# ScalarE scales the recurrence's keys as it evicts the projections, and two more tensors go through DRAM

## What is computed

```python
r, k, v = einsum(x_rkv, w_rkv)
w = -softplus(-(w0 + tanh(mix(3) @ w1) @ w2)) - 0.5
a = sigmoid(a0 + (mix(4) @ a1) @ a2)
g = sigmoid(mix(5) @ g1) @ g2
kk = heads(k * k_k)
kk = kk * rsqrt(max(sum(kk * kk), 1e-24))
k = k * (1.0 + (a - 1.0) * k_a)
y = _wkv7_scan(heads(r), exp(-exp(w)), heads(k), heads(v), kk, heads(a))
```

## Time and profile before

| what | us |
|---|---|
| median of the three runs | 2966.8 |
| lowest and highest run | 2958.1, 2972.0 |
| span of the profiled execution | 2962.6 |
| of it the projections of layer 1 | about 370 |
| of it the recurrence, from the first load to the last z | about 501 |
| busy: TensorE, VectorE, Pool, ScalarE | 2651.2, 1679.0, 1251.1, 931.4 |

### The profile page before, as it was taken

One profiled execution on the slowest core, in us unless ns is written; L12 is line 12 of the kernel. 1 busy time (PEld: TensorE's weight loads), 2 busy tenths in 40 slices (PEclk: granted clock), 3 DMA queues, 4 the chain that ended last, 5 costly groups with the idle time before them and its releaser, 6 DMA issues. The chain is left out here.

```text
span 2962.6 us, 48409 instructions
## 1 busy us (share of the span) xinstructions
PE 2651.2 (89%) x20064; PEld 2172.5 (73%) x20064; DVE 1679.0 (57%) x2078; ACT 931.4 (31%) x1551; POOL 1251.1 (42%) x630
## 2 busy tenths in 40 slices
PE   1887888999999999989989488888799999999999
PEld 1565667788887788767778377777687888788887
DVE  6745455655554633467963689998435443433434
ACT  2434433321224222154544233333234222222221
POOL 2532234444445444344433334444355444444443
PEclk9989999999999999999999799999899999999999
DMA  6421224354533222256566444433232233223333
GB/s 244 159 82 37 93 79 156 128 178 157 184 128 100 86 93 99 81 147 167 146 171 157 107 96 98 98 90 82 87 123 91 86 107 93 92 93 100 99 96 124
DMA packets 299001, 343.32 MB, mean 116 GB/s; under 512 B 214560, under 2 KB 214688, under 8 KB 298784
## 3 DMA queue, kind: packets, MB, share of 16 engines
q1 hardware_dynamic: 298784, 340.23, 38.1%
HBM read 298.29 MB, written 40.89 MB: 114 GB/s over the span
## 5 line engine op out<-in xcount | busy, mean ns | idle before, releaser
L709 POOL TENSOR_TENSOR wl<-w,wh 128x1024 fp32r<-128x1024 f32 x367 | 906.3, 2475 | 1274.8 <-ACT wh L750 1274.6
L180 PE MATMUL ps<-hi,wh 128*128 128x512 f32 x2208 | 883.6, 400 | 22.3 <-ACT qk_raw L787 10.4
L182 PE MATMUL ps<-hi,wl 128*128 128x512 f32 x2208 | 868.7, 393 | 0.0
L181 PE MATMUL ps<-lo,wh 128*128 128x512 f32 x2208 | 868.5, 393 | 0.0
L750 ACT ACTIVATE wh<-w 128x1024 fp32r<-128x1024 f32 x367 | 387.0, 1056 | 703.9 <-DMA w<-in_ffn_w_in 528.0
L1021 DVE SCALAR_TENSOR_TENSOR xt<-ps,mod,xt 128x512 f32<-128x512 f32 x384 | 286.6, 750 | 411.0 <-PE ps L182 404.5
L180 PEld LDWEIGHTS ps<-hi,wh 128*128 128x128 f32 x2208 | 420.3, 190 | 125.2 <-issue 33.8
L181 PEld LDWEIGHTS ps<-lo,wh 128*128 128x128 f32 x2208 | 421.0, 191 | 90.3 <-issue 3.7
L182 PEld LDWEIGHTS ps<-hi,wl 128*128 128x128 f32 x2208 | 419.6, 190 | 89.9
L1026 DVE TENSOR_TENSOR act<-ps,silu 128x512 f32<-128x512 f32 x88 | 60.9, 692 | 461.3 <-PE ps L182 461.3
L180 PE MATMUL ps<-act_hi,wh 128*128 128x512 f32 x704 | 282.4, 401 | 18.5 <-DVE act_lo L1030 10.0
(11 more groups left out here) (221 smaller groups left out, 3319.6 us busy)
## 6 DMA issues: line engine op xcount, KB each, us to landing
w<-in_ffn_w_in SPq DMA_DIRECT2D x176, 512.0 KB, 3.6
piece<-in_ada_w SPq DMA_DIRECT2D x96, 512.0 KB, 5.1
w<-in_ffn_w_out SPq DMA_DIRECT2D x88, 512.0 KB, 3.6
w<-in_w_rkv SPq DMA_DIRECT2D x48, 512.0 KB, 3.9
scratch<-silu SPq DMA_DIRECT2D x48, 256.0 KB, 3.0
scratch<-act SPq DMA_DIRECT2D x48, 256.0 KB, 3.1
w<-in_wqk SPq DMA_DIRECT2D x20, 512.0 KB, 5.4
xt<-in_xT SPq DMA_DIRECT2D x4, 2048.0 KB, 10.3
```

The source lines that it names most:

```text
L180: pe.matmul(out, w_hi(k), x_hi(k), start=first and k == 0, stop=False)
L181: pe.matmul(out, w_hi(k), x_lo(k), start=False, stop=False)
L182: ins = pe.matmul(out, w_lo(k), x_hi(k), start=False, stop=last and k == kc - 1)
L709: pool.tensor_tensor(wl[n % NW][:, :, :], wr[n % NW][:, :, :], wh[n % NW][:, :, :].bitcast(F32), ALU.subtract).then_inc(*wlo.up)
```

## The change

The products of the recurrence's keys with vectors move to the eviction of the projections.

In the projections: a k tile is evicted twice by ScalarE, once multiplied by `k_k` into the buffer `sq` and once plain; SyncE writes both, the first to `scratch` part 6. An a tile (`lora2`, `n % 3 == 1`) is evicted through the sigmoid, then, after a wait for that result, ScalarE makes (a * k_a - k_a) in a second buffer `a_gain`, and SyncE writes both, the second to `scratch` part 7. The two `a_gain` buffers are `total[0]` and a new tile. Buffers are free again when all writes from them have landed (`kept_before` counts them). VectorE makes -k_a once at the start.

In the recurrence: `begin` is gone from VectorE and `keys` from Pool. SyncE loads kk ready made right behind r, and `a_gain` into k2 right behind v. VectorE makes k2 = (a_gain + 1) * k in one instruction, `keys(x)`, right behind `bounded(x)`. `squares`, `decayed` and `bonus_terms` wait for both loads of the r semaphore, and `by_token(x, 0)`, `bonus_value` and `keys` for both of the v semaphore.

```diff
@@ projections: SyncE
 sp.dma_start(scratch_of(n % 3, n // 3, j), sg[i % 2]...).then_inc(*kept[i % 2].up)
+if n % 3 == 1:
+    sp.dma_start(scratch_of(6, n // 3, j), sq[i % 2]...).then_inc(*kept[i % 2].up)
...
 sp.dma_start(scratch_of(3 + n % 3, n // 3, j), af[i % 2]...).then_inc(*kept_lora[i % 2].up)
+if n % 3 == 1:
+    sp.dma_start(scratch_of(7, n // 3, j), a_gain[i % 2]...).then_inc(*kept_lora[i % 2].up)
@@ projections: ScalarE
-act.wait_ge(*kept[(n - 1) % 2].at((n - 1) // 2))
+act.wait_ge(*kept[(n - 1) % 2].at(kept_before(n - 1)))
+if idx[0] == 1:
+    act.wait_ge(*add_done.at(KC * len(plan.norms)))
+    col = V_KK + idx[1]
+    act.activation(sq[(n - 1) % 2][:, :], ps[:, bank, :], ACT.Copy, scale=vec[:, col:col + 1])
 act.activation(sg[(n - 1) % 2][:, :], ps[:, bank, :], ACT.Copy).then_inc(*taken.up)
...
-act.wait_ge(*kept_lora[m % 2].at(m // 2))
+act.wait_ge(*kept_lora[m % 2].at(kept_before(m)))
-if n % 3 < 2:
+if n % 3 == 1:
+    act.wait_ge(*ang_step.at(1))
+    act.wait_ge(*t_done.at(KC * (len(plan.norms) - 1)))
+    act.activation(af[m % 2][:, :], ps[:, 5 + m % 2, :], ACT.Sigmoid, bias=vec[:, col:col + 1]).then_inc(*a_done.up)
+    act.wait_ge(*a_done.at(KC * (n // 3) + j + 1))
+    act.activation(a_gain[m % 2][:, :], af[m % 2][:, :], ACT.Identity, scale=vec[:, V_KA + j:V_KA + j + 1],
+                   bias=minus_ka[:, j:j + 1]).then_inc(*taken_lora.up)
+elif n % 3 == 0:
@@ recurrence: SyncE
-sp.dma_start(rt[:, :, :], scr[0, bass.ds(ch, 1)]...).then_inc(*g["r_in"].up)
+for n, x in ((0, rt), (6, kk)):
+    sp.dma_start(x[:, :, :], scr[n, bass.ds(ch, 1)]...).then_inc(*g["r_in"].up)
...
+def load_key_gains(ch):
+    sp.wait_ge(*g["kb_done"].at(ch))
+    sp.wait_ge(*g["rk_done"].at(ch))
+    settle(sp)
+    sp.dma_start(k2[:, :, :], scr[7, bass.ds(ch, 1)]...).then_inc(*g["v_in"].up)
...
-    load_values(w)
+    load_values(w), load_key_gains(w)
@@ recurrence: Pool
-def keys(ch):
-    pool.wait_ge(*g["t1_done"].at(ch + 1))
-    pool.tensor_tensor(k2[:, :, :], k2[:, :, :], column(V_KA), ALU.mult).then_inc(*g["ka_step"].up)
-    pool.wait_ge(*g["ka_step"].at(ch + 1))
-    pool.tensor_tensor(k2[:, :, :], k2[:, :, :], kt_[:, :, :], ALU.add).then_inc(*g["k2_done"].up)
...
-    normed_keys(x), keys(x), bonus_terms(x)
+    normed_keys(x), bonus_terms(x)
@@ recurrence: ScalarE
 def squares(ch):
-    act.wait_ge(*g["kk_done"].at(ch + 1))
+    act.wait_ge(*g["r_in"].at(2 * (ch + 1)))
@@ recurrence: VectorE
-def begin(ch):
-    dve.wait_ge(*g["tiles_in"].at(3 * ch + 3))
-    dve.wait_ge(*g["kb_done"].at(ch))
-    dve.wait_ge(*g["rk_done"].at(ch))
-    dve.tensor_tensor(kk[:, :, :], kt_[:, :, :], column(V_KK), ALU.mult).then_inc(*g["kk_done"].up)
-    dve.scalar_tensor_tensor(k2[:, :, :], at_[:, :, :], 1.0, kt_[:, :, :], ALU.subtract,
-                             ALU.mult).then_inc(*g["t1_done"].up)
+def keys(ch):
+    dve.wait_ge(*g["v_in"].at(2 * (ch + 1)))
+    dve.scalar_tensor_tensor(k2[:, :, :], k2[:, :, :], 1.0, kt_[:, :, :], ALU.add, ALU.mult).then_inc(*g["k2_done"].up)
 def decay_sums(ch):
+    dve.wait_ge(*g["tiles_in"].at(3 * ch + 3))
     dve.tensor_tensor_scan(flat(lcum[:, :, :]), reset[:, :], flat(st_[:, :, :]), 0.0, ...)
...
-    bounded(x)
+    bounded(x), keys(x)
...
-    if w is not None:
-        begin(w)
```

## The result

The changed kernel takes 2972.1 us (median of 16 runs, 2963.2 to 2978.0) where the kernel before takes 2961.6 (16 runs, 2955.9 to 2972.0). The medians lie 10.5 us apart; the ratio of the runs is 1.0029, 95% interval 1.0019 to 1.0039, so the changed kernel is slower by 8.6 us (5.6 to 11.6). Forecast were 8.1 us less, 2958.7. The time lies within the range and within 0.5% of the forecast, but it moved the other way. That it lies so near is in part luck: the forecast started from the median of three runs, 2966.8, and the median of all sixteen, these three among them, is 5.2 us lower.

What follows compares the result with a forecast made beforehand. VectorE was taken to set the recurrence's period, except a 7.42 us TensorE stretch, and TensorE the projections. Recurrence -12.4, projections +4.2, -k_a +0.1 gave -8.1: from 2966.8 to 2958.7 us, range 2944 to 2974.

Steps and rivals of the forecast that it cites:

- The k tiles' second eviction, costed at nothing: Projections: ScalarE evicts 16 k tiles twice, 0.69 us each, between its waits while TensorE has banks to fill: 0 us.
- The bursts, +4.2: Projections, eight a evictions in each half: slower two-buffer round loses 2.6 us in the first, 1.6 in the second; bounds 1 and 12.
- the bursts become DMA-bound: Rival, projections: 32.2 us of transfers in 26.0; 6.2 us a burst plus 2.6 behind, twice, lose 17.6: 2972; chance 0.13.
- Full periods at full clock, -0.85 each: Recurrence, VectorE: `begin` gone saves 1.39 us, `keys` adds net 0.54, so a period loses 0.85; bounds 0.58 and 1.39.
- Eleven periods: -9.4: Recurrence: the 0.85 us gain of a full period, carried over all eleven full periods, gives -9.4 us.
- the recurrence was to give 12.4: Recurrence in sum: -9.4 + 0.55 + 1.0 - 5.0 + 0.5 = -12.4 us.
- Late loads, +1.0: Recurrence: new loads of kk and gains mostly hidden, SyncE free before `blocks_back` is due: +1.0 us in all (0 to 8).
- First periods -5.0, last +0.5: Recurrence: first four periods gain 5.0 us (bounds -2 and -9); the period after the last w pays 0.54 for `keys`.
- the four rivals: Bursts are free (0.22), VectorE's relief shows (0.08), bursts become DMA-bound (0.13), loads are late (0.07); the forecast itself had 0.50.
- late loads: Rival, recurrence: kk or gains land 1 us after they are wanted and the period gains nothing: 2966 to 2968; chance 0.07.
- VectorE's relief: Recurrence, lines 1802 to 1867: 2.2 us less VectorE work, costed at nothing; rival that it shows, 24 us: 2934, chance 0.08.
- The rule of the Trainium skill's "DMA: Bandwidth & Descriptors": Projections' scratch writes under 512 bytes: at full weight 1.2 us a write instead of 0.91, about 6 us more, sum about 2965.

Runs made afterwards that it cites:

- early_fill: `early` with VectorE's last inversion step moved ahead of `centre` and the block images sent earlier: 2944.6 us, 0.9940 of the kernel before.
- rec_alone: Changed recurrence behind the projections of the kernel before, its two new loads reading k and a instead: 2960.4 us, 0.9993 of the kernel before.
- early: Changed kernel with kk and gains loaded behind k, a and decay, not behind r and v, and `keys` before `bounded`: 2962.2 us, 1.0002.
- act_fill: `act_rec` plus VectorE's last inversion step moved ahead of `centre`, block images sent earlier: 2940.9 us, 0.9928 of the kernel before.
- front_alone: Changed projections with the recurrence of the kernel before, which does not read parts 6 and 7: 2969.9 us, 1.0030 of the kernel before.
- act_rec: Projections of the kernel before; ScalarE makes kk and gains inside the recurrence, rest as in `early`, no new tensors or loads: 2959.9 us, 0.9994.

## Why the prediction was wrong, step by step

- **The k tiles' second eviction, costed at nothing: wrong.** The argument looked at ScalarE's time alone. Two of the eight evictions of each half fall into the stretch of the a tiles, and their writes onto the same DMA queue; without eviction and write 6.6 us come back. Which of the two costs is not separated.
- **The bursts, +4.2: the mechanism was right, the size was not.** The round of two buffers set the a tiles' pace, as worked out; the evictions spread over 26.1 and 25.7 us where 23.9 were forecast. The sum took eviction and writes of the a tiles alone, and left out the k tiles' writes among them. TensorE idled 4.0 us where a stall of 1.3 was worked out. Together with the step above, 11.4 for 4.2. The rival "the bursts become DMA-bound" came near to what happened: its 6.2 us a burst were 6.0 and 5.6, and the DMA share rose to 0.93 and 0.96, but the 2.6 us behind each burst that make its 17.6 did not come. The Identity took 0.82 us where 0.72 were taken from the earlier trace rows, whose line passes a column of biases and none of scales; it loaded no table.
- **Full periods at full clock, -0.85 each: right, and a little too small.** The one such period takes 25.83 for 27.0, 1.17 less. Lines 1757 and 1760 (1778 and 1781 after) fell to 0.68 as forecast. `keys` took 1.35 beside Pool (1.17 assumed), line 1859, which is line 1838 of before, fell to 0.58 as forecast, and the wait before `centre` (line 1888) grew to 2.5 us on average, as forecast. That TensorE sets the stretch there is right too; the hole is where `early_fill` found room.
- **"Eleven periods: -9.4": the step that failed most.** It carried the granted clock of before over to the new kernel. TensorE now waits for the images, 23.6 us over the full periods in place of 8.0, and ten periods of eleven run with part of their matmuls at the lower level. The measured sum is -0.6, and over the other executions of the same recurrence 298.2 to 303.7 us in place of about 303: nowhere -9.4. Whole runs say the same of the stage: `rec_alone` gained 2 us where the recurrence was to give 12.4.
- **Late loads, +1.0: wrong in kind.** I asked whether SyncE's queue was free for `blocks_back`, and it was, but not the DMA engines behind it; and I had the images due at 1845.2 as an issue, not as a round trip that TensorE waits for. The two loads cost 3.9 us in the old kernel.
- **First periods -5.0, last +0.5.** The four leading periods took 3.9 us less, but the first kk landed late (ScalarE's first square waited 6.7 us), so the recurrence began 2.65 later; the end took 2.55 less. All in all -3.8 where -4.5 stood: near, but of one execution.
- **The chances.** Of the four rivals two (DMA-bound bursts, late loads) turned out to hold a part of the truth, and they add up: both cost. The forecast treated them as apart. VectorE's relief did not show in the changed kernel; its 27.6 us went into the wait before `centre`. The rule of the Trainium skill's "DMA: Bandwidth & Descriptors", Specifications, on writes below 512 bytes gave 2965, nearer to the result. No run here changes the rows' length, so what of the 11.4 us is its doing stays open. (The flat slices of the earlier trace rows read 287 to 291 GB/s, not 283; nothing hangs on it.)

What stays open: which waits bring the clock down. After 1.88 us at `level_x` it stayed up in the changed kernel, after 2.23 (in `early`, the period at 1907.40) it fell, and in `act_fill`, where no wait for `diag` is left, waits for VectorE of up to 2.34 us stand in periods at full clock and waits of 1.80 to 2.50 us in periods at the lower one; the earlier trace rows show 2.13 us at the same place at full clock. In `front_alone` three periods at the lower level had waits for `diag` of 0.41, 0.60 and 0.68 us and, just behind them, waits for VectorE of 1.56 to 1.95 us. So the images' wait alone does not settle it. The Trainium skill's "TensorE: Matmul & The Clock Gate", HAM oscillation — how this bites in real kernels, describes the pattern: a wait for data between short runs of matmuls lets the clock fall each time, and the next run starts slow. The rows agree in so far as the clock falls in or behind such waits, and do not give a length at which it turns.

## What to carry to other kernels

Work that is taken off an engine may have been the cover of a round trip: ask what ran between the send and the first reader, and if the trip gets bare, move the sender up into the idle time that the same change has opened. Write traffic has a schedule of its own: two additions that are each hidden can meet in one stretch of the DMA queue, so add up bytes by stretch and not by edit. And before a period's gain at full clock is multiplied by the number of periods, ask whether TensorE now waits where it did not: its clock is part of the price.

## What the runs showed of the hardware

- ScalarE's Identity from SBUF to SBUF with a column of scales and one of biases takes 0.81 to 0.82 us for 128 x 512; the one of the earlier trace rows, with a column of biases alone, takes 0.72.
- Sixteen activations of 128 x 64 cost ScalarE 4.6 us, 0.29 each (`act_rec`).
- Two loads of 256 KB a chunk whose data nobody reads cost 3.9 us (1.2 to 6.5) over sixteen chunks (`before_loads`). They stand ahead of transfers of 64 and 128 KB that TensorE waits for, and that wait grew from 8.0 to 14.8 us over the full periods.
- A period of the same 615 recorded matmuls takes 25.2 or 27.0 us in one execution (`early_fill`). Most of the difference is the granted clock, 1.00 or 0.94: TensorE is busy 22.4 or 24.0 us.
